# Differential attention scores: two 64-row tiles with three products each in place of a stacked contraction over 128 rows

## The chip, the cores and the metric

One Trainium2 chip, of which the kernel uses one core. The metric is the device time of one execution in microseconds (us); the kernel before has a median of 1838.38 us in three runs.

## The reference, cut to what matters

The layer normalises its input, projects it to a matrix-LSTM branch and an attention branch, and merges the two. The change touches the attention branch alone, and there only the scores. There are 8 heads; each has two components of 64 dimensions, a sequence of 1024 and blocks of 128 queries.

```python
def _diff_attention(q, k, v, lam):
    # q, k: (B, H, 2, S, dh); v: (B, H, S, 2*dh); here H=8, S=1024, dh=64
    scale = dh ** -0.5
    def block(qblk):                       # 128 queries
        s = jnp.einsum('bhcqd,bhckd->bhcqk', qblk, k).astype(jnp.float32) * scale
        p = jax.nn.softmax(s, axis=-1)
        a = p[:, :, 0] - lam * p[:, :, 1]  # component 0 less lambda times component 1
        return jnp.einsum('bhqk,bhke->bhqe', a, v.astype(jnp.float32))
```

float32 is kept by splitting each operand into a high part (type fp32r) and a low part (what the high part leaves), and by summing the products high*high, high*low and low*high.

## The kernel before

Everything is written out by hand, engine by engine, with semaphores; the order in the program of an engine is the order in which it works. The stages are: preparation, four mLSTM heads (to 710 us of the trace), eight attention heads (717 to 1435 us), and the merge with the output projection.

**An attention head.** The projections of one head put q in `qkf[:, 0]` and k in `qkf[:, 1]`, both 128 x 1024: rows 0 to 63 are component 0, rows 64 to 127 component 1. After the rotary step (POOL, and DVE for the first k) the parts are made. `k_high` and `q_high` (ACT, L1732 and L1737) write the high parts, `k_low` and `q_low` (DVE, L1290 and L1296) the low parts, and each of the four takes two instructions of 64 x 1024, one per component. They write into stacks: for component c, `qs[:, c]` holds the high part of q in the component's own 64 rows and the low part in the other 64, and `ks[:, c, b]` holds the high (b = 0) or low (b = 1) part of k in its own rows. The other 64 rows of `ks` are filled by `double_keys` (SP's queue, L452), a copy by DMA from rows to rows, 512 KB each, two per head. A matmul over all 128 rows with `ks[:, c, 0]` then gives high*high and low*high at once, the one with `ks[:, c, 1]` high*low and low*low.

**A block of queries.** `a_scores(h, q)` (PE, L794) makes the scores of one block of 128 queries against 1024 keys: 2 components x 2 halves of the keys x 2 matmuls, 8 in all, into PSUM banks 2 and 3 (component 0) and 4 and 5 (component 1). It signals `a_score` after each component. `maxima` (DVE, L1362) takes the row maximum of each component, `exps` (ACT, L1818) the exponentials with their sums, `mix` (DVE, L1349 to L1356) the weighted difference. `mix_round` (PE, L802) transposes the mixed probabilities, four 128 x 128 tiles a round in two rounds, all through PSUM bank 6; `high_round` (ACT, L1823) and `a_low_round` (DVE, L1367) read each round out as high and low part. So round 1 can't begin before DVE has read out round 0. `pv` (PE, L620) multiplies with v for every second block.

The block loop of PE, for q = 0 to 7:

```python
mix_round(h, q, 0)
if q + 1 < ST: a_scores(h, q + 1)        # the next block's scores
mix_round(h, q, 1)
...  # then a filler: 24 matmuls of the next head's projections (L612); pv(h, q // 2) behind it for odd q
```

The fillers keep PE in work while DVE and ACT do softmax. Around the end of a head, DVE's order is: low round 0 of block 7, `k_low` of component 1, low round 1, `q_low` twice, `o_out_gate` (L1385, L1387), `o_out_low` (L1392), `o_square` (L1378), then the maxima of the next head. POOL splits the weights of the fillers, two instructions per tile (L549, L552), as soon as PE has finished the tile that last used the buffer. PE's first `a_scores` of a head waits for `q_low` and for both copies of `double_keys`.

## Time and profile before

| | before |
|---|---|
| median of 3 runs | 1838.38 us (1838.1 to 1838.51) |
| span of the profiled execution, first to last instruction | 1836.2 us |
| PE busy in the span | 1684.0 us (92%) |
| DVE busy | 1185.4 us (65%) |
| ACT busy | 755.2 us (41%) |
| POOL busy | 615.8 us (34%) |
| the L794 matmuls: busy, count, mean of one | 140.3 us, 512, 418 ns |
| mean granted TensorE clock | 0.967 of full speed |

PE is the engine of matmuls, PEld its weight loads, which overlap the matmuls; DVE is the vector engine, ACT the scalar engine, POOL GpSimd, SP the sync engine that issues most DMAs. The profiled execution is one run; its span stands 2.2 us below the median of the runs, since the latter also counts what lies around the first and last instruction. A matmul's duration is its latency; in a stream, matmuls start closer together than that, so times on PE are best read from start to start.

### The profile page before, as it was taken

To read this page: it belongs to the slowest core of one execution; us is meant where nothing else is said; L and a number is where in the kernel's file an instruction comes from. 1 tells how busy PE (TensorE), PEld (TensorE's weight loads), DVE (VectorE), ACT (ScalarE), POOL (GpSimd) and SP (SyncE) were. 2 spreads that over 40 slices of the span, in tenths; PEclk is the share of its full clock that TensorE was granted. 3 is DMA by queue.
4 is the path that set the end of the run, shared out by engine and by line. 5 is a ranking of instruction groups with operands and counts; after the bars stand their busy time and mean duration, and the time that the engine had idled before them with its cause. 6 is when DMAs were issued, how large, how long until landed. Compare 5 with 4: busy or idle time off the path is not lost.

```text
span 1836.2 us, 24023 instructions
## 1 busy us (share of the span) xinstructions
PE 1684.0 (92%) x8235; PEld 1380.2 (75%) x8235; DVE 1185.4 (65%) x1740; ACT 755.2 (41%) x1462; POOL 615.8 (34%) x302
## 2 busy tenths in 40 slices
PE   4999998998998998999999989999989999998895
PEld 3778877877877876877777777787777788886784
DVE  6712777777777777787788788778787202666413
ACT  4212444443443443454545454545454113333322
POOL 2232223223223224525162525252521234443330
PEclk9999999999999998999999999999999999999998
DMA  4031111112112113121212121212121636522322
GB/s 160 23 104 35 35 47 58 34 39 64 34 33 70 35 32 95 29 58 35 58 34 57 34 57 34 57 40 51 51 58 57 220 135 211 191 79 85 121 69 91
DMA packets 137299, 129.07 MB, mean 70 GB/s; under 512 B 5089, under 2 KB 120354, under 8 KB 136226
## 3 DMA queue, kind: packets, MB, share of 16 engines
q1 hardware_dynamic: 130594, 111.66, 21.0%
q10 hardware_dynamic: 6656, 16.78, 2.3%
q8 instruction: 29, 0.48, 0.1%
q14 instruction: 20, 0.16, 0.0%
HBM read 90.67 MB, written 29.36 MB: 65 GB/s over the span
## 4 chain that ended last, share of the span: by engine, by line
PE 54%; DVE 25%; issue 10%; ACT 9%; DMA 1%; DVEq 1%; ACTq 0%; SPq 0%
PE ps L612 39%; PE ps L620 7%; PE ps L794 3%; PE ps L802 2%; DVE negmax L1362 2%; ACT probs L1818 2%; DVE q_stack L1296 2%; ACT aT_split L1823 1%; DVE o_out L1385 1%; DVE f_work L1459 1%; DVE raw_b L1029 1%; DVE mix L1354 1%; DVE aT_split L1367 1%; DVE sigmoid_work L1029 1%; DMA v_f<-in_x 1%
## 5 line engine op out<-in xcount | busy, mean ns | idle before, releaser
L612 PE MATMUL ps<-xn_split,w_split 128*128 128x512 f32 x4224 | 1047.2, 404 | 16.0 <-ACT f_branch L1518 7.3
L612 PEld LDWEIGHTS ps<-xn_split,w_split 128*128 128x128 f32 x4224 | 799.5, 191 | 205.8 <-issue 9.1
L549 POOL TENSOR_TENSOR w_split<-w_raw,ones 128x1024 fp32r<-128x1024 f32 x104 | 218.2, 2098 | 1086.7 <-PE ps L612 1028.7
L552 POOL TENSOR_TENSOR w_split<-w_raw,w_split 128x1024 fp32r<-128x1024 f32 x104 | 274.8, 2642 | 8.2
L1818 ACT ACTIVATE probs<-ps,negmax 128x1024 f32<-128x1024 f32 x128 | 142.9, 1117 | 142.2 <-DVE negmax L1362 142.2
L612 PE MATMUL ps<-h_split,w_split 128*128 128x512 f32 x768 | 182.9, 398 | 2.7 <-ACT f_branch L1518 2.6
L612 PEld LDWEIGHTS ps<-h_split,w_split 128*128 128x128 f32 x768 | 144.4, 189 | 38.4 <-ACT f_branch L1518 3.1
L1362 DVE TENSOR_REDUCE negmax<-ps 128x1 f32<-128x1024 f32 x128 | 150.6, 1215 | 4.8 <-PE ps L794 4.6
L794 PE MATMUL ps<-k_stack,q_stack 128*128 128x512 f32 x512 | 140.3, 418 | 13.7 <-DVE q_stack L1296 12.8
L1367 DVE TENSOR_TENSOR aT_split<-ps,aT_split 128x512 fp32r<-128x512 f32 x128 | 88.4, 691 | 88.0 <-ACT aT_split L1823 86.9
L794 PEld LDWEIGHTS ps<-k_stack,q_stack 128*128 128x128 f32 x512 | 95.6, 197 | 33.5 <-DMA k_stack<-k_stack 8.5
L802 PE MATMUL ps<-ident,mix 128*128 128x128 f32 x512 | 81.1, 282 | 36.6 <-DVE mix L1356 19.8
L802 PEld LDWEIGHTS ps<-ident,mix 128*128 128x128 f32 x512 | 59.6, 143 | 64.4 <-DVE aT_split L1367 31.9
L620 PEld LDWEIGHTS ps<-aT_split,va_split 128*128 128x128 f32 x768 | 95.1, 191 | 10.5 <-issue 6.9
L620 PE MATMUL ps<-aT_split,va_split 128*128 128x256 f32 x768 | 98.6, 285 | 2.2 <-DVE aT_split L1367 1.6
L1457 DVE SCALAR_TENSOR_TENSOR f_work<-qk_f 128x1024 f32<-128x1024 f32 x16 | 34.1, 2133 | 84.7 <-DMA qk_f<-spill_g 84.5
L1356 DVE SCALAR_TENSOR_TENSOR mix<-probs,rden,mix 128x1024 f32<-128x1024 f32 x64 | 82.2, 1285 | 2.3
L1823 ACT ACTIVATE aT_split<-ps 128x512 fp32r<-128x512 f32 x128 | 75.7, 591 | 12.3 <-PE ps L802 10.5
L1518 ACT ACTIVATE v_f<-ps 128x512 f32<-128x512 f32 x56 | 33.3, 596 | 84.6 <-PE ps L612 67.1
L562 POOL TENSOR_TENSOR qk_f<-qk_f,cos 128x512 f32<-128x512 f32 x30 | 38.9, 1298 | 82.1 <-DVE raw_a L1273 47.3
L1459 DVE SCALAR_TENSOR_TENSOR f_work<-qk_f,f_work 128x1024 f32<-128x1024 f32 x16 | 30.4, 1899 | 47.0 <-ACT f_work L1935 47.0
L1489 DVE TENSOR_TENSOR y_f<-ps,f_work 128x512 f32 x16 | 10.4, 687 | 65.0 <-PE ps L896 64.9
(243 smaller groups left out, 1975.2 us busy)
## 6 DMA issues: line engine op xcount, KB each, us to landing
w_raw<-in_w_in SPq DMA_DIRECT2D x80, 512.0 KB, 4.1
k_stack<-k_stack SPq DMA_DIRECT2D x16, 512.0 KB, 4.2
spill_a<-o_split SPq DMA_DIRECT2D x32, 256.0 KB, 2.9
h_split<-spill_m SPq DMA_DIRECT2D x8, 1024.0 KB, 6.9
qk_f<-spill_g SPq DMA_DIRECT2D x16, 512.0 KB, 3.4
xn_split<-spill_a SPq DMA_DIRECT2D x8, 1024.0 KB, 6.1
spill_g<-qk_f ACTq DMA_DIRECT2D x12, 512.0 KB, 2.6
spill_m<-hT_split ACTq DMA_DIRECT2D x8, 512.0 KB, 2.8
```

The lines of the kernel that those rows point to most:

```text
L549: pool.tensor_tensor(wsp[b][:, 0], raw[b][:], ones[:, 0:1].unsqueeze(2).to_broadcast([P, KT, P]), ALU.mult).then_inc(w_split, 1)
L552: pool.tensor_tensor(wsp[b][:, 1], raw[b][:], wsp[b][:, 0].bitcast(F32), ALU.subtract).then_inc(w_split, 1)
L612: mm = pe.matmul(ps[:, half, :], wsp[b][:, wl, k, :], moving[:, xl, k, cols], start=(k == 0 and n == 0), stop=(k == KT - 1 and n == 2))
L620: mm = pe.matmul(dst, st(a), mv(b), start=(start and n == 0), stop=(stop and n == 2))
L794: mm = pe.matmul(ps[:, 2 + 2 * c + i, :], qs[:, c, q * P:(q + 1) * P], ks[:, c, b, i * HALF:(i + 1) * HALF], start=(b == 0), stop=(b == 1))
L802: mm = pe.transpose(ps[:, 6, n * P:(n + 1) * P], src, ident[:])
L1356: dve.scalar_tensor_tensor(am[b][:], pr[:, 1], rden[:, 1, 0:1], am[b][:], ALU.mult, ALU.add).then_inc(a_mix.sem, 1)
L1362: dve.tensor_reduce(nmax[:, q % 2, c:c + 1], ps[:, 2 + 2 * c:4 + 2 * c, :].rearrange("p b k -> p (b k)"), AX_X, ALU.max, negate=True).then ...
L1367: dve.tensor_tensor(dst(1), ps[:, 6, :].rearrange("p (k s) -> p k s", k=4), dst(0).bitcast(F32), ALU.subtract).then_inc(a_tr_read.sem, 1)
L1459: dve.scalar_tensor_tensor(fw[:], z, 0.0, fw[:], ALU.min, ALU.subtract).then_inc(f_logsig, 1)
L1818: act.activation(pr[:, c], ps[:, 2 + 2 * c:4 + 2 * c, :].rearrange("p b k -> p (b k)"), ACT.Exp, bias=nmax[:, b, c:c + 1], accum_out=den[: ...
L1823: act.activation(dst, ps[:, 6, :].rearrange("p (k s) -> p k s", k=4), ACT.Copy).then_inc(a_tr_hi.sem, 1)
```

## The change

- `qs` becomes `[high | low]` of q, `ks` `[high | low]` of k, both 128 x 2 x 1024 with each component in its own 64 rows. The doubled rows are gone, and with them `double_keys`, its two DMAs per head and the semaphore `k_doubled`.
- A matmul of `a_scores` contracts 64 rows: rows 0 to 63 for component 0, rows 64 to 127 for component 1. There are 2 halves x 3 products x 2 components = 12 for each block in place of 8; component is the innermost loop, so neighbours use different rows and different PSUM banks. Both components' `a_score` signals come from the last two matmuls.
- The wait for `a_exp` is now one, for component 1, ahead of all twelve.
- The high and low parts are each made by one instruction of 128 x 1024 in place of two of 64 x 1024. `k_low` stands in block 6, `q_low` in block 7 behind low round 1; `q_high` in block 7 between the two high rounds.

```diff
-        qs = sb("q_stack", [P, 2, S], F32R, at=a_scope)
-        ks = sb("k_stack", [P, 2, 2, S], F32R, at=a_scope)
+        qs = sb("aq_split", [P, 2, S], F32R, at=a_scope)
+        ks = sb("ak_split", [P, 2, S], F32R, at=a_scope)
...
-            def double_keys(hh):
-
-                own = (slice(0, AD), slice(AD, P))
-                for c in range(2):
-                    sp.wait_ge(a_qk_lo.sem, a_qk_lo.after(hh, c))
-                    sp.dma_start(ks[own[1 - c], c].bitcast(F32), ks[own[c], c].bitcast(F32)).then_inc(k_doubled, 16)
-
             def a_tiles(h, first):
 
                 for j, c in enumerate((C_AQ, C_AK, C_AV, C_AZ)):
                     load_weights(G_A, 4, h, j, w_in_v, c + P + h * P)
-                    if j == (1 if first else 2):
-                        double_keys(h)
...
                 if q == 0:
-                    pe.wait_ge(k_doubled, 32 * h + 32)
-                    pe.wait_ge(a_qk_lo.sem, a_qk_lo.after(h, 3))
-                for c in range(2):
-                    if q > 0:
-                        pe.wait_ge(a_exp.sem, a_exp.after(h, 2 * (q - 1) + c))
-                    elif not is_zero(h):
-                        pe.wait_ge(a_exp.sem, a_exp.after(h, c) - 2)
-                    for i in range(2):
-                        for b in range(2):
-                            mm = pe.matmul(ps[:, 2 + 2 * c + i, :], qs[:, c, q * P:(q + 1) * P],
-                                           ks[:, c, b, i * HALF:(i + 1) * HALF], start=(b == 0), stop=(b == 1))
-                    mm.then_inc(a_score.sem, 1)
+                    pe.wait_ge(a_qk_lo.sem, a_qk_lo.after(h, 1))
+                if q > 0:
+                    pe.wait_ge(a_exp.sem, a_exp.after(h, 2 * (q - 1) + 1))
+                elif not is_zero(h):
+                    pe.wait_ge(a_exp.sem, a_exp.after(h, 1) - 2)
+                for i in range(2):
+                    for n, (a, b) in enumerate(PASSES):
+                        for c in range(2):
+                            rows = slice(c * AD, (c + 1) * AD)
+                            mm = pe.matmul(ps[:, 2 + 2 * c + i, :], qs[rows, a, q * P:(q + 1) * P],
+                                           ks[rows, b, i * HALF:(i + 1) * HALF], start=(n == 0), stop=(n == 2))
+                            if i == 1 and n == 2:
+                                mm.then_inc(a_score.sem, 1)
...
-            def q_low(hh, c):
-
-                dve.wait_ge(a_qk_hi.sem, a_qk_hi.after(hh, 2 + c))
-                dve.tensor_tensor(qs[own[1 - c], c], qkf[own[c], 0], qs[own[c], c].bitcast(F32),
-                                  ALU.subtract).then_inc(a_qk_lo.sem, 1)
+            def q_low(hh):
+
+                dve.wait_ge(a_qk_hi.sem, a_qk_hi.after(hh, 1))
+                dve.tensor_tensor(qs[:, 1], qkf[:, 0], qs[:, 0].bitcast(F32), ALU.subtract).then_inc(a_qk_lo.sem, 1)
```

PE, an attention head's block loop; `ps<-ident,mix` is `mix_round`, `ps<-ident,v_f` the transposes of v, and L612 or L600 the filler. Before:

```order
L802 MATMUL ps<-ident,mix 128x128 [waits a_tr_read,a_mix]
L802 MATMUL ps<-ident,mix 128x128 x3
L794 MATMUL ps<-k_stack,q_stack 128x512 [waits a_exp]
L794 MATMUL ps<-k_stack,q_stack 128x512 x3
L794 MATMUL ps<-k_stack,q_stack 128x512 [waits a_exp]
L794 MATMUL ps<-k_stack,q_stack 128x512 x3
L802 MATMUL ps<-ident,mix 128x128 [waits a_tr_read]
L802 MATMUL ps<-ident,mix 128x128 x3
```

The same place in the changed kernel:

```order
L791 MATMUL ps<-ident,mix 128x128 [waits a_tr_read,a_mix]
L791 MATMUL ps<-ident,mix 128x128 x3
L782 MATMUL ps<-ak_split,aq_split 128x512 [waits a_exp]
L782 MATMUL ps<-ak_split,aq_split 128x512 x11
L791 MATMUL ps<-ident,mix 128x128 [waits a_tr_read]
```

Nothing moved against its neighbours; eight became twelve, and the second wait in the middle is gone.

DVE, the end of a head: low round 0 and 1 (`aT_split`), the low parts, then the output gate. Before:

```order
L1290 TENSOR_TENSOR k_stack<-qk_f,k_stack 64x1024 [waits a_qk_hi]
L1367 TENSOR_TENSOR aT_split<-ps,aT_split 128x4x128 [waits a_tr_hi]
L1290 TENSOR_TENSOR k_stack<-qk_f,k_stack 64x1024 [waits a_qk_hi]
L1367 TENSOR_TENSOR aT_split<-ps,aT_split 128x4x128 [waits a_tr_hi]
L1296 TENSOR_TENSOR q_stack<-qk_f,q_stack 64x1024 [waits a_qk_hi] x2
L1385 TENSOR_TENSOR o_out<-o_f,o_rs 128x256 [waits a_olo,a_rs]
L1387 TENSOR_TENSOR o_out<-o_out,gate_a 128x256 [waits a_ost]
```

The same place in the changed kernel:

```order
L1276 TENSOR_TENSOR ak_split<-qk_f,ak_split 128x1024 [waits a_qk_hi]
L1350 TENSOR_TENSOR aT_split<-ps,aT_split 128x4x128 [waits a_tr_hi] x2
L1281 TENSOR_TENSOR aq_split<-qk_f,aq_split 128x1024 [waits a_qk_hi]
L1368 TENSOR_TENSOR o_out<-o_f,o_rs 128x256 [waits a_olo,a_rs]
L1370 TENSOR_TENSOR o_out<-o_out,gate_a 128x256 [waits a_ost]
```

The second `k_low` between the two low rounds and the second `q_low` ahead of the output gate are gone.

## Rows read from the trace of the kernel before

**Rows 1.** The page's part 1: engines over the span.

```profile
PE 1684.0 (92%) x8235; PEld 1380.2 (75%) x8235; DVE 1185.4 (65%) x1740; ACT 755.2 (41%) x1462; POOL 615.8 (34%) x302
```

**Rows 2.** The timeline (start us, us, engine, line; last, idle before it) of one block.

```profile
1057.56 1.69 PEld L794 LDWEIGHTS ps<-k_stack,q_stack 128*128 128x128 f32 x8
1057.59 2.09 PE L794 MATMUL ps<-k_stack,q_stack 128*128 128x512 f32 x8
...
1059.11 2.35 DVE L1362 TENSOR_REDUCE negmax<-ps 128x1 f32<-128x1024 f32 x2
1059.29 0.59 PEld L802 LDWEIGHTS ps<-ident,mix 128*128 128x128 f32 x4
...
1060.36 1.11 ACT L1818 ACTIVATE probs<-ps,negmax 128x1024 f32<-128x1024 f32 x1 [1.89 <-DVE negmax L1362]
...
1064.29 1.28 DVE L1356 SCALAR_TENSOR_TENSOR mix<-probs,rden,mix 128x1024 f32<-128x1024 f32 x1
...
1065.76 0.59 PEld L802 LDWEIGHTS ps<-ident,mix 128*128 128x128 f32 x4
```

**Rows 3.** The timeline of a long stream of full-array matmuls.

```profile
692.66 17.89 PE L612 MATMUL ps<-xn_split,w_split 128*128 128x512 f32 x76
```

**Rows 4.** PE and PEld around the only matmuls of 36 rows (L662, L668).

```profile
131.64 0.86 PE L612 MATMUL ps<-xn_split,w_split 128*128 128x512 f32 x3
132.42 1.86 PEld L662 LDWEIGHTS ps<-row_decay,pick 36*128 36x128 f32 x16 [0.36 <-issue]
136.63 1.04 PE L668 MATMUL ps<-ident,row_f 36*128 36x36 f32 x8
137.60 0.93 PEld L612 LDWEIGHTS ps<-xn_split,w_split 128*128 128x128 f32 x3
```

**Rows 5.** The timeline where a head ends and the next begins.

```profile
1070.04 4.05 DVE L1296 TENSOR_TENSOR q_stack<-qk_f,q_stack 64x1024 fp32r<-64x1024 f32 x2
1070.13 2.88 POOL L549 TENSOR_TENSOR w_split<-w_raw,ones 128x1024 fp32r<-128x1024 f32 x1 [17.29 <-PE ps L612]
...
1070.14 3.13 PE L620 MATMUL ps<-aT_split,va_split 128*128 128x256 f32 x24
...
1073.10 3.25 POOL L552 TENSOR_TENSOR w_split<-w_raw,w_split 128x1024 fp32r<-128x1024 f32 x1
1074.13 2.50 DVE L1385 TENSOR_TENSOR o_out<-o_f,o_rs 128x256 f32<-128x256 f32 x1
1074.23 1.68 PEld L794 LDWEIGHTS ps<-k_stack,q_stack 128*128 128x128 f32 x8 [1.16 <-issue]
...
1076.66 0.43 DVE L1387 TENSOR_TENSOR o_out<-o_out,gate_a 128x256 f32<-128x256 f32 x1
...
1084.28 1.28 DVE L1356 SCALAR_TENSOR_TENSOR mix<-probs,rden,mix 128x1024 f32<-128x1024 f32 x1
...
1085.68 0.42 PEld L802 LDWEIGHTS ps<-ident,mix 128*128 128x128 f32 x4 [3.28 <-issue]
```

**Rows 6.** L1296's durations (ns: minimum, median, maximum).

```profile
L1296 DVE TENSOR_TENSOR q_stack<-qk_f,q_stack x16: 1219/2658/3248, 711.6 to 1341.1; 64x1024 fp32r<-64x1024 f32 x16
```

**Rows 7.** The timeline where the first attention head begins.

```profile
707.68 2.14 ACT L1732 ACTIVATE k_stack<-qk_f 64x1024 fp32r<-64x1024 f32 x2 [7.69 <-DVE qk_f L1284]
...
710.63 2.36 POOL L549 TENSOR_TENSOR w_split<-w_raw,ones 128x1024 fp32r<-128x1024 f32 x1 [4.07 <-PE ps L612]
711.56 5.79 DVE L1296 TENSOR_TENSOR q_stack<-qk_f,q_stack 64x1024 fp32r<-64x1024 f32 x2 [0.32 <-ACT q_stack L1737]
...
717.47 3.06 PEld L794 LDWEIGHTS ps<-k_stack,q_stack 128*128 128x128 f32 x8 [7.35 <-DMA k_stack<-k_stack]
...
721.29 1.23 DVE L1362 TENSOR_REDUCE negmax<-ps 128x1 f32<-128x1024 f32 x1 [0.48 <-PE ps L794]
...
725.99 1.28 DVE L1356 SCALAR_TENSOR_TENSOR mix<-probs,rden,mix 128x1024 f32<-128x1024 f32 x1
727.66 0.59 PEld L802 LDWEIGHTS ps<-ident,mix 128*128 128x128 f32 x4
```

More of the change, by code:

```diff
@@ L330, in hybrid_block @@
         rope_k0 = sem("rope_k0")
-        a_qk_hi = signal("a_qk_hi", 4)
-        k_doubled = sem("k_doubled")
-        a_qk_lo = signal("a_qk_lo", 4)
+        a_qk_hi = signal("a_qk_hi", 2)
+        a_qk_lo = signal("a_qk_lo", 2)
         a_score = signal("a_score", 16)
@@ L1273, in shuffle @@
                     dve.stream_shuffle((rawa, rawb)[n // 2][:, cols], qkf[:, n // 2, cols], swap).then_inc(shuf_done, 1)
-            own = (slice(0, AD), slice(AD, P))
             def rope_first_k():
@@ L1336, in m_head @@
                     k_low(0)
-                    for c in range(2):
-                        q_low(0, c)
+                    q_low(0)
             with dve.Fori(0, MH - 1) as h:
@@ L1404, in a_head @@
                         maxima(h, q + 1)
-                    elif not last:
-                        k_low(h + 1, (1,))
                     a_low_round(h, round_of(q, 1), at_dst(q, 1))
@@ L1410, in a_head @@
                     elif not last:
-                        for c in range(2):
-                            q_low(h + 1, c)
+                        q_low(h + 1)
                     if q == 0:
@@ L1423, in a_head @@
                     if not last and q == 6:
-                        k_low(h + 1, (0,))
+                        k_low(h + 1)
                     if q in (2, 4):
@@ L1721, in m_step @@
                     act.activation(cs[:, 0], cf[:], ACT.Copy).then_inc(chi_done.sem, 1)
-            own = (slice(0, AD), slice(AD, P))
             def k_high(hh):
@@ L1730, in k_high, with q_high @@
                     act.wait_ge(rope_done, 3 * (4 * hh + 3) + 3)
-                for c in range(2):
-                    act.activation(ks[own[c], c, 0], qkf[own[c], 1], ACT.Copy).then_inc(a_qk_hi.sem, 1)
-            def q_high(hh, comps=(0, 1)):
-                for c in comps:
-                    act.activation(qs[own[c], c], qkf[own[c], 0], ACT.Copy).then_inc(a_qk_hi.sem, 1)
+                act.activation(ks[:, 0], qkf[:, 1], ACT.Copy).then_inc(a_qk_hi.sem, 1)
+            def q_high():
+                act.activation(qs[:, 0], qkf[:, 0], ACT.Copy).then_inc(a_qk_hi.sem, 1)
             def read_rope(base, per_head, h, hh, n, half):
                 if half == 0 and not is_zero(hh):
-                    act.wait_ge(a_qk_lo.sem, a_qk_lo.after(hh, 3) - 4)
+                    act.wait_ge(a_qk_lo.sem, a_qk_lo.after(hh, 1) - 2)
                 read_half(base, per_head, h, (4 if is_zero(hh) else 0) + n // 2, half,
@@ L1803, in m_head @@
                     act.wait_ge(rope_done, 3 * 1 + 3)
-                    q_high(0)
+                    q_high()
                     read_v(1, 1)
@@ L1878, in a_head @@
                     elif not last:
-                        q_high(h + 1, (0,))
+                        q_high()
                     high_round(h, round_of(q, 1), at_dst(q, 1))
-                    if q == 7 and not last:
-                        q_high(h + 1, (1,))
                     if q + 1 < ST:
```

10 lines of the change are left out of this document (3 added, 7 removed).

## The prediction, made before the changed kernel ran

> **What bounds the kernel now.** I read the page's engine shares first [rows 1]: PE is busy 92% of the span, so time saved on PE pays only where PE is not waiting. The change lives in the attention stage, so I took its timeline, one block and one head boundary.
>
> In a block [rows 2] call T the first L794 weight load, 1057.56. PE does 8 score matmuls, then round 1 of the transposes (weights at T+1.73), filler and `pv`. DVE meanwhile runs a chain: row maxima from T+1.55 (behind low round 0; component 0 first), exponentials from T+2.80, ACT having waited 1.89 us for the maxima, `mix` until 1064.29 + 1.28 = T+8.01. PE loads for the next round 0 at 1065.76, 0.19 behind the end of `mix`. Where PE does wait for `mix` the distance is 0.12 (1085.56 to 1085.68) [rows 5], so this block has 0.07 us of slack. Softmax and PE are co-critical: whatever delays the maxima by over 0.07 us lengthens the block.
>
> At a head boundary [rows 5] PE waits twice: 1.16 us for `q_low`, and 3.28 us before the first round 0, which ends 11.5 us after the first scores began. There DVE is the bound: `q_low` takes 4.05 us for two, `o_out` (L1385) 2.50. The shortest L1296 took 1.22, the median 2.66 [rows 6]. POOL's L549 runs 1070.13 to 1073.01 and L552 1073.10 to 1076.35; the second `q_low` ends 1.1 behind the first POOL instruction, the first `o_out` 0.28 behind the second. So these DVE and POOL instructions take turns.
>
> **Part by part.**
>
> *Fewer low parts at the seven boundaries.* Before, DVE and POOL alternate: `q_low`, L549, `q_low`, L552, L1385, L1387, until 1077.09. After, one 1.22 us instruction of 128 rows (time goes by columns, as in the 128-row rows) ends at 1071.26; L549 follows to 1073.0; L1385 ends about 0.3 later, 1073.3; L552, asked for at 1073.1, takes its usual 2.2 to about 1075.5; L1387 ends 0.28 behind it at 1075.75. Gain 1.34. All that follows (output split, maxima, exponentials, `mix`, round 0 at 1085.68) hangs on L1387, so the boundary gains 1.34, bounds 0.9 (POOL gets in ahead of `q_low`, 0.09 us away) and 2.8 (no turn lost, the whole second `q_low`). PE's own wait of 1.16 goes, too: `pv`'s last matmul starts at 1070.14 + 3.13 - 0.28 = 1072.99. That is PE time DVE still hides. The second `k_low` stood where DVE waits for ACT anyway: nothing. 7 x 1.34 = **-9.4**.
>
> *The start of the first head* [rows 7]. PE sits idle 7.35 us until 717.47. ACT makes two `k_high` (2.14 us), then v, then `q_high`; DVE two `q_low` in 5.79, behind POOL's L549 and L552. With one `k_high` all of ACT comes 1.07 earlier: `q_high` 709.40 to 710.45, `q_low` starts 710.49, POOL's L549 only at 710.63. So `q_low` ends at 711.71 and PE starts at 711.8, 5.65 earlier. The old scores, after the long idle, took 3.06 us of loads against 1.69 in rows 2 in the same eight; now the idle ahead of them is short, and I take the 1.7 of rows 2. Maxima of component 1 then start at 711.8 + 1.7 + 1.1 = 714.65, and from there to round 0 takes 727.27 - 721.29 + 0.12 = 6.1: 720.75 against 727.66. **-6.9**. If POOL wins the race by those 0.14 us, 2.4 less.
>
> *The doubling copies.* They are waited for at the same places; behind `q_low` they cost nothing beside it. Gone with it.
>
> *The scores.* This is the unknown. A full matmul takes (17.89 - 0.39) / 75 = 0.233 us from start to start [rows 3], so the eight end their starts 0.11 + 7 x 0.233 = 1.74 after the first load (2.09 - 0.39 = 1.70 in rows 2). The 12 half-height ones: no row has two row tiles at work at once. Bounds: one slot a pair (6 x 0.233) and one slot each (12 x 0.233). I take the pair, because neighbours use disjoint rows of the array and different banks, and because the two weight loads of a pair fit: loads of 36 rows follow each other by (1.86 - 0.19) / 15 = 0.111 [rows 4], two of them 0.222 < 0.233. The Trainium skill ("TensorE: Matmul & The Clock Gate", Part 3) states that matmuls on distinct row groups run concurrently; no row here shows it. Last start after the first load: 0.11 + 0.11 + 5 x 0.233 = 1.39, 0.35 less than before.
>
> *Switching between array shapes.* Rows 4 are the only places where matmuls of 36 rows meet full ones. The last full one starts at 131.64 + 0.86 - 0.39 = 132.11, the next load only at 132.42: 0.31 later, with nothing to wait for ("issue"), where in rows 2 it starts with the last matmul. On the way back, 137.37 to 137.60: 0.23. So a switch lets the array run empty: 0.21 of streaming plus 0.10. This is what the Trainium skill says ("TensorEngine Tiling (Array Packing)", Key Properties: changing the tiling mode drains the engine), and the trace agrees. Behind a transposing matmul (0.11) I take 0.21, bounds 0 and 0.31. Each block pays twice. In: the first score load at T+0.21. Out: last start T+0.21+1.39 = T+1.60, load at T+1.91, first transposing matmul T+1.97; before T+1.73 and, behind the last stream, T+1.96. For PE a wash: 0.36 won, 0.36 lost.
>
> *The signals.* Component 0 used to be ready after 4 matmuls; now it is the 11th. Ready at T + 0.21 + 0.11 + 5 x 0.233 + 0.39 + 0.04 = T+1.92, so the maxima start 0.36 later than T+1.55. That is a new wait on DVE, with ACT and `mix` queued behind it. It counts in blocks whose maxima start so early: q = 0, 4 and 6 of a head (0.36, and 0.29 each where 0.07 is slack). In the others DVE comes later anyway (gate, output, v), or `pv` gives over 2 us of slack. 0.94 x 8 heads = **+7.5**, bounds 0 (switches free and shorter latency) and 12.
>
> *Sum:* -9.4 - 6.9 + 7.5 = -8.8 on the profiled 1836.2, so 1827.4 of span; on the median 1838.4 it gives **1829.6**.
>
> **Rivals.**
> 1. *No drain at the switches.* Ready T+1.71, delay 0.15, 0.31 a head: +2.5. Total -13.8: 1824.6. Against it: rows 4, where the 0.31 us has no other reason.
> 2. *A weight load waits for the matmul in its own rows.* A pair then costs 0.233 + 0.11 = 0.34; component 0 is ready at T+2.45, delay 0.9: 0.90 + 0.83 + 0.83 in those three blocks, 0.48 in block 5, 0.39 on PE in block 3 = 3.4 a head, +27. Total **+11: 1849**, slower. It decides from a pair of about 0.28 us on. The Trainium skill has such a rule (same page, "What overlaps and what doesn't": loads overlap matmuls in flight only where the row group differs). Against it: in rows 2 and 3 loads run beside full-array matmuls in the same rows, or the slot could not be 0.233.
> 3. *The row tiles don't overlap at all*, so the change doesn't do what it says. Ready at T+3.08, delay 1.5 in three blocks, 1.1 in blocks 3 and 5, 0.3 in block 1: 7 a head, +56. Total +40: 1878.
>
> **How the numbers follow.** Forecast 0.66 (own range: 1821, boundaries at 2.8 with half the delays, to 1836, race lost and delays at 12); rival 1 0.08; rival 2 0.12; rival 3 0.09; 0.05 between pairs of 0.25 and 0.33 (1832 to 1846). The range 1821 to 1850 takes in all but rival 3 and some tails. A measurement can tell about 0.2%, 3.7 us, from no change. Faster, below 1834.7: 0.62 of the forecast's 0.66 and rival 1, 0.70; same: the other 0.04 and 0.03 of the between cases, 0.07; slower: rivals 2 and 3 and the rest, 0.23.
>
> **What would show it.** Pairs: L782's twelve start within 1.4 to 1.6 us of the first load (rival 2: 2.0; rival 3: 2.7), and the partner of a pair about 0.11 behind. Switch: load of the first score matmul 0.2 behind the last transposing start, and 0.31 on the way out. Signals: a new wait of DVE's maxima for PE, about 0.3 us in three blocks a head. Boundary: one aq_split row of 1.22, L1370 (now L1387's work) ending 1.3 earlier, round 0 still waiting for DVE. First head: scores at about 711.8. I'm wrong if the twelve take over 1.9 us, or if q_low loses the race with POOL.

## The result, and the profile after

The changed kernel takes **1849.55 us** (median of 4 runs, 1848.79 to 1852.22) against 1838.38 before: ratio 1.0064, 95% interval 1.005 to 1.0078. It is slower, by 11 us, where the forecast was 9 us faster. The profiled execution has a span of 1847.0 us against 1836.2.

All below is read from the two traces. Part 1 of the page of the changed kernel answers to [rows 1]: every engine has less work than before, and yet the span is longer.

```profile
span 1847.0 us, 24420 instructions
PE 1681.5 (91%) x8491; PEld 1356.0 (73%) x8491; DVE 1181.1 (64%) x1724; ACT 737.5 (40%) x1446; POOL 608.6 (33%) x302
```

One block on the timeline of the changed kernel (start us, us, engine, line; last, the idle time before it), the answer to [rows 2], block 5 of the fourth head (blocks counted from 0):

```profile
1038.40 0.46 PEld L791 LDWEIGHTS ps<-ident,mix 128*128 128x128 f32 x4
1038.50 0.60 PE L791 MATMUL ps<-ident,mix 128*128 128x128 f32 x4
...
1039.03 1.23 PEld L782 LDWEIGHTS ps<-ak_split,aq_split 64*128 64x128 f32 x12 [0.17 <-issue]
1039.03 1.66 PE L782 MATMUL ps<-ak_split,aq_split 64*128 64x512 f32 x12
...
1040.62 0.42 PEld L791 LDWEIGHTS ps<-ident,mix 128*128 128x128 f32 x4 [0.36 <-DVE aT_split L1350]
...
1040.72 2.36 DVE L1345 TENSOR_REDUCE negmax<-ps 128x1 f32<-128x1024 f32 x2 [0.26 <-PE ps L782]
```

The twelve half-height matmuls are over 1.66 us after T = 1039.03; less the 0.39 of the last one, the last starts at T+1.27. The next load is at T+1.59, the maxima at T+1.69. So row tiles work side by side, scores take less of PE than before (T+1.70 for the last start), and the maxima start 0.14 us later behind the load than the T+1.55 of [rows 2]. The load itself now stands 0.20 us behind the last transposing start, where before it stood with it; counted from that start, the maxima are 0.34 us late.

**Where the 11 us went.** I took the first score load of each of the 64 blocks in both traces and compared the 63 steps between them. The numbers are us, summed over the heads; a step "4" leads from block 4 to block 5 of a head, "7" to the next head. The last three columns belong to experiments below.

| step | changed − before | component by component − changed | both edits − changed | both edits: changed − before |
|---|---|---|---|---|
| to the first scores | −5.2 | −2.1 | −2.8 | −8.8 |
| 0 | −0.8 | −1.7 | −17.2 | −1.4 |
| 1 | +6.1 | +5.7 | −7.7 | +2.7 |
| 2 | +3.2 | −3.7 | −7.2 | −0.1 |
| 3 | +0.4 | −1.7 | −0.1 | +0.3 |
| 4 | +2.6 | −0.6 | −2.6 | 0.0 |
| 5 | +0.9 | +2.7 | 0.0 | +0.9 |
| **6** | **+12.2** | **−12.2** | **−12.2** | 0.0 |
| 7 | −7.8 | +2.3 | −0.1 | −3.6 |
| behind the last scores | −1.0 | +1.0 | 0.0 | +0.7 |
| total | +10.8 | −10.2 | −49.9 | −9.3 |

(Only seven steps "7". Each column compares one profiled execution of either kernel. The first row has a spread of its own: seven kernels with the changed parts and twelve scores a block, which do the same work up to there, have their first scores between 709.41 and 712.40 us.) Steps 2, 4 and 6 together cost 18.0 us; all three are the same event, as the timelines below show for step 6. It is in all eight heads in step 6, in two more heads than before in step 2 and in the last head in step 4. The step that costs most is step 6: 1.62 us in seven heads, 0.93 in the last. Here is the timeline where it begins, of the kernel before, in the fourth head (the scores of block 6, T = 1048.57; the gate product is the one that DVE does in its block 5 step for the output pair of blocks 2 and 3):

```profile
1047.74 0.42 DVE L1385 TENSOR_TENSOR o_out<-o_f,o_rs 128x256 f32<-128x256 f32 x1
1048.19 0.42 DVE L1387 TENSOR_TENSOR o_out<-o_out,gate_a 128x256 f32<-128x256 f32 x1
1048.48 1.90 POOL L549 TENSOR_TENSOR w_split<-w_raw,ones 128x1024 fp32r<-128x1024 f32 x1 [2.73 <-PE ps L612]
1049.24 0.59 ACT L1823 ACTIVATE aT_split<-ps 128x512 fp32r<-128x512 f32 x1
```

and the same place in the changed kernel (T = 1047.90; L1368 and L1370 are the old L1385 and L1387, L537 is POOL's old L549):

```profile
1047.11 0.42 DVE L1368 TENSOR_TENSOR o_out<-o_f,o_rs 128x256 f32<-128x256 f32 x1
1047.37 1.91 POOL L537 TENSOR_TENSOR w_split<-w_raw,ones 128x1024 fp32r<-128x1024 f32 x1 [2.59 <-PE ps L600]
1047.56 2.00 DVE L1370 TENSOR_TENSOR o_out<-o_out,gate_a 128x256 f32<-128x256 f32 x1
1049.68 0.42 ACT L1821 ACTIVATE o_split<-o_out 128x256 fp32r<-128x256 f32 x1 [1.76 <-DVE o_out L1370]
1050.00 0.58 ACT L1799 ACTIVATE aT_split<-ps 128x512 fp32r<-128x512 f32 x1
1051.22 2.35 DVE L1345 TENSOR_REDUCE negmax<-ps 128x1 f32<-128x1024 f32 x2
1051.35 0.42 PEld L791 LDWEIGHTS ps<-ident,mix 128*128 128x128 f32 x4 [2.22 <-DVE aT_split L1350]
```

Before, DVE's gate product started 0.29 us ahead of POOL's weight split and took its usual 0.42. Now it starts 0.19 behind it, and is over only at 1049.56, 0.28 behind the end of the split: the same 0.28 as at the head's end in [rows 5]. Behind it ACT's output copy, `aT_split` (queued behind that copy), and the maxima are all late: T+3.32, before T+1.90. The by-line rows (instructions, busy us, mean ns of one) say how often:

```profile
L1387 DVE TENSOR_TENSOR o_out<-o_out,gate_a 128x256 f32<-128x256 f32 x32 | 19.9, 622 | 1.1
```

before, and after:

```profile
L1370 DVE TENSOR_TENSOR o_out<-o_out,gate_a 128x256 f32<-128x256 f32 x32 | 51.7, 1617 | 1.1
```

Before, 4 of the 32 are wide (about 2 us); after 22: this one in all eight heads, those of the seven head ends (where the wide one used to be L1385 alone), and seven others.

**The head's start** (steps 0 and 1) has a second loss. The timeline and the windows (stretch, its length, busy us of PE, PEld, DVE, ACT, POOL with counts, then the granted clock) of the changed kernel, at block 1 of the fifth head:

```profile
1085.17 0.95 PE L791 MATMUL ps<-ident,mix 128*128 128x128 f32 x4 [2.82 <-DVE mix L1339]
1086.05 2.21 PEld L782 LDWEIGHTS ps<-ak_split,aq_split 64*128 64x128 f32 x12 [0.33 <-issue]
1088.99 2.36 DVE L1345 TENSOR_REDUCE negmax<-ps 128x1 f32<-128x1024 f32 x2 [1.51 <-PE ps L782]
```

```profile
1085.70:1089.20 3.50, 3.50 (x17) 2.15 (x17) 0.90 (x2) 0.60 (x1) 0.00 (x0) 0.56 0.00 0
```

and the same stretch before:

```profile
1086.07 1.68 PEld L794 LDWEIGHTS ps<-k_stack,q_stack 128*128 128x128 f32 x8
```

```profile
1085.70:1089.20 3.50, 3.50 (x20) 2.97 (x21) 2.19 (x3) 1.10 (x3) 0.00 (x0) 1.00 0.00 0
```

In this head PE, after 2.82 us without a matmul (3.21 without a weight load), gets 0.56 of its clock, near the lower of its two levels (1.2 GHz), and block 1's maxima wait until T+2.94. Block 1's scores are stretched so in 6 of the 8 heads after, in 4 before. That the change itself brought these two more is not shown: run 2 has its row tiles and as long an idle time, and one such head.

### The profile page after: what moved, and what is told of

Read it like the earlier page. It is cut to its first block, busy times and chain, and to the rows that moved or that the text cites. A ratio compares the mean times of both kernels' runs of the same rounds, so it can differ in the third digit from the quotient of the medians.

```text
span 1847.0 us, 24420 instructions
## 1 busy us (share of the span) xinstructions
PE 1681.5 (91%) x8491; PEld 1356.0 (73%) x8491; DVE 1181.1 (64%) x1724; ACT 737.5 (40%) x1446; POOL 608.6 (33%) x302
## 4 chain that ended last, share of the span: by engine, by line
PE 50%; DVE 28%; issue 10%; ACT 10%; DMA 1%; DVEq 1%; ACTq 0%; SPq 0%
PE ps L600 35%; PE ps L608 6%; ACT probs L1794 3%; DVE negmax L1345 3%; PE ps L782 3%; DVE o_out L1370 3%; PE ps L791 2%; DVE mix L1337 1%; ACT aT_split L1799 1%; DVE o_out L1368 1%; DVE aT_split L1350 1%; DVE f_work L1439 1%; DVE raw_b L1018 1%; DVE sigmoid_work L1018 1%; DVE mix L1339 1%
## 5 line engine op out<-in xcount | busy, mean ns | idle before, releaser
L600 PE MATMUL ps<-xn_split,w_split 128*128 128x512 f32 x4224 | 1050.2, 405 | 16.0 <-ACT f_branch L1498 7.3
L600 PEld LDWEIGHTS ps<-xn_split,w_split 128*128 128x128 f32 x4224 | 801.8, 192 | 206.6 <-issue 9.1
L537 POOL TENSOR_TENSOR w_split<-w_raw,ones 128x1024 fp32r<-128x1024 f32 x104 | 217.4, 2090 | 1100.5 <-PE ps L600 1042.9
L540 POOL TENSOR_TENSOR w_split<-w_raw,w_split 128x1024 fp32r<-128x1024 f32 x104 | 268.7, 2583 | 8.1
L600 PE MATMUL ps<-h_split,w_split 128*128 128x512 f32 x768 | 181.8, 396 | 2.9 <-ACT f_branch L1498 2.6
L600 PEld LDWEIGHTS ps<-h_split,w_split 128*128 128x128 f32 x768 | 143.3, 188 | 38.6 <-ACT f_branch L1498 3.1
L791 PE MATMUL ps<-ident,mix 128*128 128x128 f32 x512 | 85.2, 291 | 61.3 <-DVE aT_split L1350 40.0
L782 PE MATMUL ps<-ak_split,aq_split 64*128 64x512 f32 x768 | 113.1, 429 | 1.0 <-DVE aq_split L1281 1.0
L782 PEld LDWEIGHTS ps<-ak_split,aq_split 64*128 64x128 f32 x768 | 71.7, 197 | 25.3 <-issue 10.3
L1370 DVE TENSOR_TENSOR o_out<-o_out,gate_a 128x256 f32<-128x256 f32 x32 | 51.7, 1617 | 1.1
```

The lines of the kernel that those rows point to most:

```text
L537: pool.tensor_tensor(wsp[b][:, 0], raw[b][:], ones[:, 0:1].unsqueeze(2).to_broadcast([P, KT, P]), ALU.mult).then_inc(w_split, 1)
L540: pool.tensor_tensor(wsp[b][:, 1], raw[b][:], wsp[b][:, 0].bitcast(F32), ALU.subtract).then_inc(w_split, 1)
L600: mm = pe.matmul(ps[:, half, :], wsp[b][:, wl, k, :], moving[:, xl, k, cols], start=(k == 0 and n == 0), stop=(k == KT - 1 and n == 2))
L782: mm = pe.matmul(ps[:, 2 + 2 * c + i, :], qs[rows, a, q * P:(q + 1) * P], ks[rows, b, i * HALF:(i + 1) * HALF], start=(n == 0), stop=(n == 2))
L791: mm = pe.transpose(ps[:, 6, n * P:(n + 1) * P], src, ident[:])
L1370: dve.tensor_tensor(ost[:], ost[:], ga[:, 2 * n * P:2 * (n + 1) * P], ALU.mult).then_inc(a_ost.sem, 1)
```

## The experiments

The theory: **DVE and POOL take turns** on their large SBUF products, and the change moved PE (which releases POOL) and DVE against each other so that DVE's gate products now come second. The rivals: **the row tiles** cost by themselves (drains at switches, late signal of component 0), or the changed low parts do. Each kernel ran beside the kernel before, whose median was 1838.2 to 1838.8 us. Some of the expectations count by PE's loop, whose pass q issues the scores of block q + 1: their "block 4" gate product, and the block that takes 10.6 us in place of 9.0, belong to step 6 of the table.

### 1. The parts without the row tiles

Eight full-array score matmuls from the new parts, with a wait and a signal for each component as before the change; the scores are not the reference's, all else is computed.

```diff
-                for i in range(2):
-                    for n, (a, b) in enumerate(PASSES):
-                        for c in range(2):
-                            rows = slice(c * AD, (c + 1) * AD)
-                            mm = pe.matmul(..., qs[rows, a, ...], ks[rows, b, ...], ...)
...
+                for c in range(2):
...
+                    for i in range(2):
+                        for b in range(2):
+                            mm = pe.matmul(..., qs[:, c, ...], ks[:, b, ...], ...)
+                    mm.then_inc(a_score.sem, 1)
```

> The change without its row tiles: the split layout, one instruction for each low and high part, no doubling copy, but the scores as 8 matmuls over all 128 rows with the two signals as before (so the two components are summed together and the scores are not the reference's). Turns theory (the loss of the change is DVE's output-gate instruction falling in behind POOL's weight split): the blocks keep their old timing, the boundary and the first head keep their gain of about 1.1 x 7 and 6.5 us, and L1370 (the gate) is slow no more often than before; 1825 us, 1822 to 1828. Switch theory (the loss is the draining of the array and the late signal of component 0): the same 1825. If it is above 1835, the parts themselves cost what the change lost.

Measured: 1820.98 us (1819.75 to 1822.8), ratio 0.9907 [0.989, 0.9924]. The smaller low parts and the missing key copy are good for 17 us, more than the forecast's 16.3 for them (−9.4 and −6.9) and 1 us below the range expected here. Step 6 is as in the kernel before (0.04 us apart over all heads). The loss comes in with the row tiles; by what way is not told by this run.

### 2. The row tiles alone

The kernel before, its stacks kept, with the scores issued as twelve half-height matmuls in pairs; the third product takes q's high part where its low part belongs, so the scores lack that share.

```diff
...
-                    for i in range(2):
-                        for b in range(2):
-                            mm = pe.matmul(..., qs[:, c, ...], ks[:, c, b, ...], ...)
...
+                for i in range(2):
+                    for n, (a, b) in enumerate(PASSES):
+                        for c in range(2):
+                            rows = slice(c * AD, (c + 1) * AD)
+                            mm = pe.matmul(..., qs[rows, c, ...], ks[rows, c, b, ...], ...)
```

> The kernel before with row tiles alone: stacks, both low parts and the doubling copies stay, the scores are 12 matmuls of 64 rows with both signals at the end (the third product reads the high part of q again in place of the low one, so low*high is left out of the result). Turns theory: scores 0.4 us shorter on PE, so POOL starts its split 0.3 us earlier than in the kernel before, and the gate in block 4 of every head falls behind it: 1.6 us in block 5 of each head, 1 to 1.7 more in the first blocks, the boundary as before: 1862 us, 1857 to 1866. Switch theory by the prediction's terms (0.94 us a head): 1846.

Measured: 1860.28 us (1856.93 to 1860.91), ratio 1.0121 [1.0104, 1.0137]. Step 6 grew by 12.2 us as in the changed kernel, step 2 by 3.2 and step 4 by 2.6. As the turns would have it:

```profile
L1389 DVE TENSOR_TENSOR o_out<-o_out,gate_a 128x256 f32<-128x256 f32 x32 | 37.3, 1167 | 1.1
```

The row "622" of before has become 1167 with nothing of DVE's or POOL's work changed.

### 3. POOL waits for one gate product

A wait on POOL ahead of its first weight split of a head, until the gate product of the timelines above is done. It covers the gate products of the first six heads.

```diff
+                if not is_zero(h):
+                    pool.wait_ge(a_ost.sem, a_ost.after(h - 1, 3))
                 split_weights(base, per_head, h, j)
```

> The changed kernel with one wait on POOL: it begins the weight split at the end of block 4 only when DVE has written the gated output of that block. Nothing is taken off PE. Turns theory: the gate takes 0.42 in place of 2.0 us there, block 5 is back at 9.0 from 10.6 us in heads 0 to 6: minus 11 us, 1838.5 (1836 to 1841). Switch theory: the gate only marks time that is lost anyway; 1849.5, unchanged within 2 us.

Measured: 1834.58 us (1833.42 to 1837.23), ratio 0.9983 [0.9973, 0.9992]; 15 us under the changed kernel, by one wait, and 1.4 us below the range expected. Its timeline in the fourth head:

```profile
1039.29 0.42 DVE L1371 TENSOR_TENSOR o_out<-o_f,o_rs 128x256 f32<-128x256 f32 x1
1039.74 0.43 DVE L1373 TENSOR_TENSOR o_out<-o_out,gate_a 128x256 f32<-128x256 f32 x1
1040.46 1.89 POOL L537 TENSOR_TENSOR w_split<-w_raw,ones 128x1024 fp32r<-128x1024 f32 x1 [3.51 <-DVE o_out L1373]
```

Step 6 gave back 1.57 us in each of the six heads that the wait covers and nothing in the others. The row tiles, their drains and the late signal are all still there. So that step is the turns' and not the array's. These 9.4 us are two thirds of the 14.5 between the two profiled spans; 1.7 came ahead of the first scores, and 3.4 in steps 0 to 3, where this execution had four heads with stretched scores and not six.

### 4. POOL waits for all three

```diff
+                if not is_zero(h):
+                    pool.wait_ge(a_ost.sem, a_ost.after(h - 1, 5))
                 split_weights(base, per_head, h, j + 1)
+                if not is_zero(h):
+                    pool.wait_ge(a_ost.sem, a_ost.after(h - 1, 7))
                 split_weights(base, per_head, h, j + 2)
```

> The changed kernel with three such waits on POOL (block 4, the head's boundary, block 0), so that DVE's gate instructions always go ahead of POOL's split. Turns theory: 11 us as in the run with one wait; at the boundary the gate ends about 3.7 us earlier, and the maxima of the next head come about 2.1 us earlier, limited by the scores: 7 x 2.1; PE idles 1 in place of 3.2 us there and keeps its clock, and the first blocks lose neither the slow scores nor the slow gate: another 9. Together 1815 us, 1808 to 1825. Switch theory: 1840 to 1850.

Measured: 1829.2 us (1827.3 to 1829.36), ratio 0.9951 [0.9934, 0.9967]: the right direction, but 14 us above what I expected and 4 above the range. The collision in blocks 0 and 1 is gone (step 2 gave 8.7 us more than in the third run, of which steps 1 and 3 took 3.2 back); at the head's end the maxima gained only 0.31 us, T+3.55 for T+3.86. Its timeline says why:

```profile
1061.67 1.90 POOL L537 TENSOR_TENSOR w_split<-w_raw,ones 128x1024 fp32r<-128x1024 f32 x1 [18.77 <-DVE o_out L1377]
1062.06 1.78 DVE L1382 TENSOR_TENSOR o_split<-o_out,o_split 128x256 fp32r<-128x256 f32 x1 [0.57 <-ACT o_split L1828]
1063.64 2.44 POOL L540 TENSOR_TENSOR w_split<-w_raw,w_split 128x1024 fp32r<-128x1024 f32 x1
1063.77 2.61 DVE L1368 TENSOR_TENSOR o_sq<-o_f 128x256 f32<-128x256 f32 x1
1066.30 2.34 DVE L1352 TENSOR_REDUCE negmax<-ps 128x1 f32<-128x1024 f32 x2
```

The split, held back behind the gate product, now meets the next two DVE instructions, the low part and the squares, and the maxima of the next head stand behind them.

### 5. The same waits on the kernel before

> The kernel before with the same three waits on POOL that took 20 us off the changed kernel (each weight split of POOL starts only when the gate product of DVE that it could meet has been issued and done). If DVE and POOL take turns and the changed kernel lost its time because its gate products now meet POOL's splits in nearly every head, the kernel before has little to win here, since only 4 of its block gate products are wide: 4 x 1.6 us, so about 1832 us (1826 to 1838), the step from a head's last block to the next head's first moved by under 1 us. If the waits help whatever the scores look like (POOL's splits always in the way of something), they are worth 20 us here too: about 1818 us.

Measured: 1838.06 us (1836.16 to 1838.77), ratio 0.9999 [0.9989, 1.0009], at the upper end of the range expected from the turns, and 6 us above its middle value. The 20 us that the waits took off the changed kernel are no general gain. The 7.0 us that steps 2 and 7 gave back were lost in steps 0 and 1: a head's first maxima stand at T+4.62 instead of T+4.23, for run 4's reason, and block 1's scores are stretched in six heads instead of four.

### 6. PE made slower: component by component

The changed kernel with the loop over c outermost, so that six matmuls of one row tile are followed by six of the other. Each component's signal now comes from its own last matmul.

```diff
-                for i in range(2):
-                    for n, (a, b) in enumerate(PASSES):
-                        for c in range(2):
...
+                for c in range(2):
...
+                    for i in range(2):
+                        for n, (a, b) in enumerate(PASSES):
...
-                            if i == 1 and n == 2:
-                                mm.then_inc(a_score.sem, 1)
+                    mm.then_inc(a_score.sem, 1)
```

> The changed kernel with the twelve score matmuls of a block issued component by component (six of component 0, then six of component 1) instead of in pairs of different rows. If two row tiles only run side by side when they stand next to each other in the queue, nothing overlaps any more: the twelve take 11 x 0.21 = 2.3 to 2.7 us instead of 1.27, component 0 is ready at about 1.5 us instead of 1.69, and a block's PE work grows by 1.0 to 1.4 us. On the path or not: if PE's length of a block counts, 1849.5 + 63 x 0.3 to 1.3 us, 1870 to 1930; if only DVE's order counts, POOL is released 1.2 us later in each block and the wide gate products of block 4 go away (as in the kernel before): 1835 to 1850.

Measured in one execution alone, so without an interval: 1838.61 us, beside 1849.55 for the changed kernel (lowest of four 1848.79). The scores take **more** of PE (last start at T+1.84 instead of T+1.27) and the kernel is 11 us **faster**. Its timeline in the fourth head:

```profile
1042.36 0.42 DVE L1367 TENSOR_TENSOR o_out<-o_f,o_rs 128x256 f32<-128x256 f32 x1
1042.81 0.42 DVE L1369 TENSOR_TENSOR o_out<-o_out,gate_a 128x256 f32<-128x256 f32 x1
1043.20 1.89 POOL L537 TENSOR_TENSOR w_split<-w_raw,ones 128x1024 fp32r<-128x1024 f32 x1 [3.41 <-PE ps L600]
1043.49 2.24 PE L782 MATMUL ps<-ak_split,aq_split 64*128 64x512 f32 x12
```

POOL is released by a later PE, and starts 0.39 us behind the start of the gate product. The moved signal has no part in it: the first maxima stand at T+1.69 and the gate product at T+8.53 in both kernels (T the first score load of block 5), and only POOL moved, from T+8.34 to T+8.92. Step 6 lost all of its 12.2 us, and the gate products' mean is 974 ns instead of 1617. What the slower PE costs is in the table, too (steps 1, 5 and 7).

### 7. The next head's maxima first, with all waits

To avoid run 4's new collision, DVE takes the next head's first maxima directly behind the last gate product; and the POOL waits are carried on into the last two heads.

```diff
...  # the waits of run 4, and those for the last two heads
             def a_head(h, first, last):
-                maxima(h, 0)
+                if first:
+                    maxima(h, 0)
...
                         o_out_gate(h, 2)
+                        if not last:
+                            maxima(h + 1, 0)
                         o_out_low(h, 2)
```

> The changed kernel with the three waits, a wait of the same kind for the splits of the last two heads, and DVE taking the next head's first two maxima directly behind the last gate product of a head, ahead of the low part of the output (L1375) and of the squares (L1361). With the waits alone those two met POOL's split at the head's end (1.78 and 2.61 us where 0.42 us is their own time), and the first maxima came 3.55 us behind the first score weight load. If that is what the boundary still costs, the maxima come at 1.7 to 1.9 us and seven boundaries give 1.8 us each, and the last two heads 1.6 us each: 1829.2 - 12.6 - 3.2, about 1814 us (1806 to 1820). If the first maxima are not on the path there (the low clock at a head's start or ACT's reading sets it), it stays within 3 us of 1829.

Measured: **1798.91 us** (1797.77 to 1800.94), ratio 0.9789 [0.9771, 0.9806], 7 us below the range expected. This beats both kernels, by 39 and 51 us, and leaves out nothing of the computation. Timeline at the head's end:

```profile
1050.12 0.43 DVE L1382 TENSOR_TENSOR o_out<-o_out,gate_a 128x256 f32<-128x256 f32 x1
1051.80 1.23 PEld L794 LDWEIGHTS ps<-ak_split,aq_split 64*128 64x128 f32 x12
1053.49 2.36 DVE L1357 TENSOR_REDUCE negmax<-ps 128x1 f32<-128x1024 f32 x2 [2.95 <-PE ps L794]
1055.76 0.42 DVE L1387 TENSOR_TENSOR o_split<-o_out,o_split 128x256 fp32r<-128x256 f32 x1
1060.72 0.42 PEld L803 LDWEIGHTS ps<-ident,mix 128*128 128x128 f32 x4 [1.05 <-issue]
```

The maxima come at T+1.69 (run 4: T+3.55), DVE is idle ahead of them, and the two products behind them take 0.42 each. PE's weight loads wait 1.05 us for the first round 0 instead of 3.21. No block of this kernel has stretched scores, where run 4 still had five. So step 0 gave 1.8 us in the seventh head, where run 4's clock had held, about the 1.86 of the maxima, and up to 2.3 where it had fallen, and step 1 another 7 us. The waits in the last two heads gave 5.2 us (steps 4 and 6) in place of 3.2. Together that is 11 of the 15 us by which the run beat what I expected.

### 8. Both edits on the kernel before

> The same edits (waits on POOL in all heads, next head's first maxima ahead of the low part and the squares) on the kernel before, full-array scores and doubled keys kept. Its first maxima stand 4.2 us behind the first score weight load and can come at 1.6 to 2.9 us; the split of POOL leaves the two q_stack subtractions alone, which may bring the head's first scores 0.9 us forward. Seven times 1.3 to 3.6 us: 1813 to 1829 us, most likely 1818. If the change itself (parts instead of stacks, row tiles, no key copy) is worth something once DVE and POOL don't meet, the changed kernel with these edits is faster than this one by the 5 to 7 us of the first head and the rest of the q and k low parts; if the row tiles cost by themselves (a shape switch in every block, a later first component), this one is level or faster.

Measured: 1807.49 us (1806.56 to 1810.16), ratio 0.9836 [0.9818, 0.9853], 5.5 us below the range expected: step 0 gave 16.6 us, and steps 1, 2 and 7 another 12.4. Once DVE and POOL don't meet, **the change is worth 8.6 us**, 1807.49 to 1798.91, where I had expected 5 to 7, and where it cost 11 us without the edits. The last column of the table has the steps.

### 9. DVE's order alone

The changed kernel with run 7's new DVE order and no waits.

> The changed kernel with DVE's new order at a head's end alone (the next head's first two maxima ahead of the low part and the squares), no wait on POOL. Between the two heads the gate products stay wide (2.12 and 2.49 us), so the maxima can come about 2.5 us behind the first score weight load instead of 3.86: 7 x 1.35 us, about 1840 us (1834 to 1846), and block 4's step stays at 10.6 us. If POOL's split were harmless and only DVE's order mattered, this alone would bring the 30 us that order and waits brought together over the waits alone: about 1819 us.

Measured: 1832.7 us (1830.97 to 1839.29), ratio 0.9977 [0.9964, 0.999]. The maxima come at T+2.42 and step 6 stays at 10.61 us, both as worked out. It is 7 us better than my middle value and 1.3 below the range, since in the profiled execution (1832.59 us) again no block has stretched scores: steps 0 and 1 gave 12.1 and 7.7 us, of which new collisions in steps 2 and 3 took 3.5 back. Only six of the ten executions ran so (1830.97 to 1832.8, mean granted clock 0.972 to 0.975); the other four took 1837.33 to 1839.29 at 0.968 to 0.970, near what I expected. A clock that fell at some heads' starts would fit, but none of the four was traced. Order alone 16.9 us, waits alone 20.4, both 50.6, of which 5.2 belong to the waits in the last two heads that run 4 did not have. The remaining 8 us or so are what each edit does by taking away what spoils the other.

### 10. Run 7 without the row tiles

> The kernel with both edits (waits on POOL, first maxima early) that took 1798.9 us, with the row tiles taken back: eight score matmuls over all 128 rows from the parts as they lie, no key copy. Its scores are not the reference's (both components' rows are summed in one product, and a product is left out); all else is computed. It tells what the row tiles are worth or cost once DVE and POOL don't meet. By the steps of the traces: the block's weight loads 0.45 us longer, component 0 ready 0.14 us sooner, no shape switch. If nothing but those two count, about 1796 us (1792 to 1800), the row tiles costing 3 us over the whole run. If PE's shorter block is what pays (0.33 us in 56 blocks and more), it is slower than 1799 by up to 18 us. If the row tiles cost by themselves what the runs without waits seemed to show (28 us between the two), about 1771 us.

Measured: 1793.91 us (1792.43 to 1794.71), ratio 0.9756 [0.9738, 0.9773]. So the row tiles themselves cost about 5 us, neither 28 nor less than nothing. Head by head it is 0.64 us in step 0, where the maxima come at T+1.25 instead of T+1.69, and 0.11 each in steps 5 and 7: 0.86 a head, 6.8 in all. (In the profiled executions its first scores started 2.5 us later than run 7's, within the spread named under the table, for which I found no cause.) It leaves a product out, so it is no version to use.

### 11. Run 7, component by component

> The same 1798.9 us kernel with the twelve score matmuls component by component. In the changed kernel without waits this order made PE's block 0.57 us longer and the run 11 us shorter. If that gain was only that POOL came 0.3 us later and so behind DVE's gate product, it is gone here, where the waits hold POOL back anyway, and the longer block costs: the steps from block 4 to 5 and 5 to 6 grew 0.3 us each, so 1799 to 1806 us, most likely 1803. If the order is better by itself (fewer stops between rows), about 1788 us.

Measured: 1808.36 us (1807.79 to 1808.83), ratio 0.9836 [0.9818, 0.9853]. The order that won 11 us now **loses 9.5**: 0.94 to 1.05 us in each head (in most heads 0.27 in step 4, 0.35 each in steps 5 and 7, nothing in step 6), 7.9 in all, 2.7 us ahead of the first scores, within the spread named under the table, and 1.2 back at the end. It is 2 us outside what I expected, and on the turns' side: with POOL held back by a wait, a slower PE only costs.

## Why the prediction was wrong, point by point

**Which step failed.** It is this one: "It counts in blocks whose maxima start so early: q = 0, 4 and 6 of a head (...). In the others DVE comes later anyway (gate, output, v)". (This q counts PE's loop: the maxima meant are those of blocks 1, 5 and 7; block 6 is among "the others".) The turns had been seen, with the numbers right ("So these DVE and POOL instructions take turns"), but only where DVE and POOL already collided, at the head's end. They weren't looked for where the two just missed each other. The gate product ahead of block 6's scores led POOL's split by 0.29 us (1048.19 and 1048.48 above), and the forecast's own delay of the maxima was 0.36, with POOL where it was: by its own numbers the product fell behind the split. The runs showed what that costs: 1.6 us a head in step 6, 12.2 in all, and with the same event in steps 2 and 4 18.0 of the 19.6 us between the forecast's −8.8 and the measured +10.8 of span. I had asked what each wait costs in its own place, not what it does to the order in which two engines ask.

**PE's share.** "For PE a wash: 0.36 won, 0.36 lost" was off as well, by less. From first to last score matmul start it is 1.27 instead of 1.70, 0.43 won; the way in cost 0.17 and the way out 0.09 more than before. So round 1 begins 0.17 sooner behind round 0, and a faster PE releases POOL sooner. Counted from block 5's T (1039.81 before, 1039.03 after), POOL came 0.33 earlier and the gate product 0.15 later, 0.48 against a lead of 0.29. Counted from the last transposing start ahead of it, which is the forecast's own T, POOL came 0.13 earlier and the product 0.35 later: the forecast delay was enough by itself. Runs 3 and 6 show each side: hold POOL back by a wait, or by a slower PE, and step 6 is as before.

**Side by side.** Right: two row tiles at once, last start at T+1.27 (1.39 forecast: neither the first matmul nor its partner starts 0.11 behind its load, but the second pair comes 0.34 behind the first and not 0.23). The Trainium skill ("TensorE: Matmul & The Clock Gate", Part 3) has matmuls in different row tiles run at once, and the trace agrees. Rivals 2 and 3 are dead: the pairs start 0.23 us apart (only the second 0.34 behind the first), and the loads of the next pair start together with the matmuls of a pair, all at T+0.34, so weights were loaded beside the matmul in their own rows. The Trainium skill ("TensorE: Matmul & The Clock Gate", "What overlaps and what doesn't") rules that out; here the trace decides. That the measured 1849.55 is the 1849 of rival 2 is chance.

**Switches.** Right: 0.20 in (0.21 forecast; 1047.70 for the last transposing start, 1047.90 for the load) and 0.31 out. Rival 1, without a drain, falls.

**The signals.** Right in size, but priced too high and in the wrong blocks. The maxima wait for PE in 0.26 us pieces, and are 0.34 late where the forecast had 0.36, both counted from the last transposing start. The forecast took 0.29 of that for block 5; step 5 grew by 0.12 (8.76 to 8.88 in the fifth head). 0.07 was slack, as forecast; most of the rest is round 0, whose four transposes behind an idle PE take 0.39 us from the first load to the last start and not 0.56. In block 1, for which the forecast took the whole 0.36, PE loaded for the next round 0 only 0.65 behind `mix` before (fifth head), where a waiting PE takes 0.12, so there was slack there, too. In a kernel without the collisions (run 10) the row tiles cost 0.86 a head, 6.8 us, where I had forecast 0.94 and 7.5. That nearness is luck: 0.64 of it is the head's first block, for which the forecast had nothing (the maxima 0.44 later behind the load, and 0.20 for the switch).

**The boundaries.** 7 x 1.34 was forecast. The timeline of the changed kernel shows the order that I had drawn up, the second gate product behind POOL's second split included:

```profile
1070.81 1.22 DVE L1281 TENSOR_TENSOR aq_split<-qk_f,aq_split 128x1024 fp32r<-128x1024 f32 x1
1071.01 2.76 POOL L537 TENSOR_TENSOR w_split<-w_raw,ones 128x1024 fp32r<-128x1024 f32 x1 [19.25 <-PE ps L600]
1071.94 2.12 DVE L1368 TENSOR_TENSOR o_out<-o_f,o_rs 128x256 f32<-128x256 f32 x1
1073.85 2.44 POOL L540 TENSOR_TENSOR w_split<-w_raw,w_split 128x1024 fp32r<-128x1024 f32 x1
1074.09 2.49 DVE L1370 TENSOR_TENSOR o_out<-o_out,gate_a 128x256 f32<-128x256 f32 x1
```

The head's first scores come 1.10 sooner behind the last block's, and round 0 another 0.36 sooner (11.09 behind the scores, 11.45 in [rows 5]): 1.46 together, near 1.34. But 0.5 of that goes back in the next score block, by the switch and the lower clock. Over the seven boundaries steps 7 and 0 gave 7.3 us in place of 9.4. The forecast had no term for the clock there, though block 1's scores were stretched in four heads before: I had looked at one boundary, a good one.

**The first head.** −6.9 forecast, −6.5 measured: the first scores 5.23 earlier (the race with POOL was won, at 710.96 against 711.37), the next step 1.27 shorter. The 5.23 has the spread of the first scores in it, up to 3 us.

**The sum.** −8.8 was forecast, and −8.6 is what the change is worth in run 8 against run 7. That agreement is partly luck: the boundaries brought 3.6 there instead of 9.4, the start of the attention stage 8.8 with up to 3 us of spread in it.

What stays open: why PE's clock falls at some heads' starts and not at others. In the fifth head it held after 3.28 us without a weight load before, and fell after 3.21 in the changed kernel. In the traces of runs 7 to 11 PE was without a matmul for at most 1.45 us ahead of block 1's scores, and they were stretched in no head; in the other eight traces it was so for 2.1 to 3.3 us (seven heads in each), and they were stretched in one to six heads. So the 6.1 us of step 1 are only in part the change's: the same step grew by 2.7 where no clock fell (last column), and the rest goes with the two more stretched heads, which another execution might not have.

## What to carry to other kernels

Before giving two engines that share a resource a new relative time, list the places where they now miss each other by less than your change moves them, not only those where they collide; a lead of 0.29 us was worth 12 us here. An order that holds by luck of timing should be made to hold by a wait on the engine with slack, and what the waiting work will then meet must be looked at next. A change should be judged again once the collision is out of the way: this one went from 11 us of loss to 8.6 us of gain.

## What the runs showed of the hardware

- A DVE product of 0.42 us (128x256, both inputs in SBUF) took 1.78 to 2.61 us when it asked behind POOL's weight split (mostly 1.9 to 2.5 us), and ended 0.28 us behind it. `TENSOR_REDUCE` from PSUM beside the same POOL instructions kept to 1.2 us each, and `aT_split`, a product with one input from PSUM, to 0.69.
- The two matmuls of a pair of row tiles start 3 ns apart in the trace's records, and so do their weight loads.
- Row tiles overlap without standing next to each other: six of one and then six of the other ended their starts at 1.84 us, not at the 11 x 0.233 = 2.6 us of one after the other; in the middle the starts are 0.117 us apart, alternating.
- From the last matmul start to the next weight load it took 0.31 us where row tiles were left behind a 512-column matmul, and 0.20 where they were entered behind a transposing one; without a switch the load stood within 0.01 us of that start in both places.
